# Two-layer decoder trunk on one core: second token tile's rows added ahead of the first tile's folding, attention's ScalarE and VectorE put into TensorE's order, inputs loaded and transposed tile by tile

## The chip, the cores and the metric

The kernel runs on one core of one Trainium2 chip. A core has TensorE (PE in the profile), VectorE (DVE), ScalarE (ACT), GpSimd (POOL) and SyncE (SP), which run their own instruction lists and meet through semaphores, and 16 DMA engines. The metric is the device time of one execution in microseconds (us). The profile is of one execution; its own time and its span are given below.

## The reference

Input x is 512 tokens by 1024 features in float32. Two layers, each a mixer and a mixture of experts (MoE), each followed by a layer norm of the residual:

```python
h = layer_norm(ALPHA * h + mixer(h)); h = layer_norm(ALPHA * h + moe(h))
```

Layer 0's mixer projects x by a 1024x1536 matrix; 512 of the columns feed a state-space branch (u), 1024 feed a gated convolution. Layer 1's mixer is a sparse attention with 16 heads over 4 key heads: per head a compressed branch (31 compressed keys), a selected branch and a window branch. With 512 positions all blocks are selected and the window covers all, so the last two are causal softmaxes over different keys and values. The MoE takes the top 8 of 64 experts plus one shared expert; every token gets eight expert rows, scaled by its gates, which are summed:

```python
y = sum over the 8 chosen experts of gate * ((silu(x @ w_gate[e]) * (x @ w_up[e])) @ w_down[e]) + shared(x)
```

## The kernel before

The program is a row of parts, each closed by a barrier: the even mixer (input projection, state space and convolution, finish), MoE layer 0, the odd mixer (input projection, compression, attention), MoE layer 1. The 512 tokens are four tiles (i = 0 to 3) of 128 partitions, all in float32. A float32 matmul stands in the profile as two MATMUL instructions.

**Input projection (`even_in_project`).** SP issues the loads in program order: the identity (first columns of the constant table), x in four tiles of 512 KB on one semaphore, the column constants, then the projection's weights in three pieces of 2 MB (`win[0]`, `win[2]`, `win[1]`, each of 512 columns), with the state matrices b and c between. PE waits for all of x, then transposes feature chunk by feature chunk over all four tiles (`emit_transposes`: eight groups of four transposes, two PSUM banks; ACT copies even chunks and DVE odd ones to `xT`), then makes twelve products of 16 MATMULs each in `order`, the first four from `win[0]`. DVE meanwhile builds tables, which PE transposes or multiplies between the later products.

**End of each MoE layer.** The expert rows were scattered to `y_dram`, eight rows per token. After the last step, SP issues 16 loads (`pieces`, 1 MB each, two of the eight rows of a tile's 128 tokens per piece, four pieces a tile, in tile order). For each tile DVE adds rows r = 0 to 3 to `g.x` (`add_row`, L850), and PE sums rows 4 to 7 in PSUM (`stored_rows`, L514) together with the rows of the last two steps, which it takes from SBUF by one-hot matmuls (`last_steps`, L522). `row_sums(i)` signals `half_done`. DVE then folds PE's sums in (L974, two instructions) and normalizes the tile (`norm.dve_tile`, with a square root on ACT). Before the loop (L968) DVE has added rows 0 to 2 of tile 0 (`EARLY` = 3). `row_sums(2)` and `row_sums(3)` wait until the banks that they reuse have been folded (L528). In layer 0 PE also transposes the normalized tiles (`turn_output`, L639); in layer 1 SP stores each tile to `out`.

**Attention (`attention`).** There are 32 units (`units`); unit n is a head pair's 128 queries, and its keys are 1, 2, 3 or 4 tiles of 128 (so unit n has "width" n % 4 + 1; the last four units run 4, 3, 2, 1). Each has four score blocks hb: two selected (hb 0, 1, in `bSel`) and two window (hb 2, 3, in `bWin`). For a block: PE makes scores, DVE adds the causal mask and takes the row minimum (`mask`, L2047), ACT takes the exponential and the row sum (L2021), DVE makes `coef` from the sums and gates (L2083), POOL scales (L1915), PE transposes (`turns`, L1954, PSUM banks `bT` in alternation, so a turn waits until the turn before the last has been copied out), ACT copies turns 0 and 2 and DVE turns 1 and 3 to `pT` (`take_turn`, L2009), and PE multiplies by the values (`values`, L1980). Once for each four units the compressed branch rides along: its scores come with the selected ones of a width-1 unit (L1932), DVE's `compressed_low` (three instructions, from L2054) and `compressed_scale` (L2067 to L2073) and one more turn (`compressed_turns`, L1962, copied by ACT at L2034) follow.

PE's order in iteration k is

```python
sel_scores(k + 1); turns(k - 2, 0); turns(k - 2, 1); compressed turn, if any
win_scores(k + 1); turns(k - 2, 2); turns(k - 2, 3); values(k - 3)
```

`sel_scores(k + 1)` waits until DVE has masked blocks 0 and 1 of unit k. ACT's order in its iteration k is the four exponentials of unit k, then turn 0 of unit k - 2, the compressed turn, turn 2. DVE's is the four masks of unit k, `coefficients(k - 1)`, then turns 1 and 3 of unit k - 2.

## Time and profile before

| | us |
|---|---|
| median of 3 runs | 2105.09 (2103.9 to 2106.59) |
| the profiled execution's own time | 2104.37 |
| its span in the trace | 2102.6 |
| PE busy | 1997.5 (95%) |
| DVE busy | 760.7 (36%) |
| ACT busy | 400.5 (19%) |
| POOL busy | 392.4 (19%) |

The granted TensorE clock averages 0.98 of full speed. The busy time of PE counts instructions whose modelled ends overlap the next one's start. The stages lie at 0 to 111 us (input projection), 113 to 207 (rest of the even mixer), 208 to 982 (MoE layer 0, its last rows from 922), 984 to 1329 (odd mixer, attention from 1142) and 1330 to 2102 (MoE layer 1, its last rows from 2040).

### The profile page before, as it was taken

How to read it: one execution, taken by the hardware profiler on the slowest of the kernel's cores; microseconds unless marked ns; L12 is line 12 of the kernel's file. 1: busy time of each engine (PE TensorE's matmuls, PEld its weight loads, DVE VectorE, ACT ScalarE, POOL GpSimd, SP SyncE). 2: the span in 40 equal slices, each digit the busy share in tenths (PEclk: the TensorE clock that was granted, in tenths of full speed). 3: DMA queues.
4: the chain of work that ended last, by engine and by line, in shares of the span. 5: the costliest groups of instructions: out<-in, count | busy, mean ns of one | idle time of the engine just before them, and what ended most of it. 6: DMA issues, size and time to landing. Idle time of an engine off the chain costs nothing. (4 is left out here: it accounts for less than half of the span.)

```text
span 2102.6 us, 26532 instructions
## 1 busy us (share of the span) xinstructions
PE 1997.5 (95%) x8566; PEld 994.1 (47%) x8566; DVE 760.7 (36%) x1957; ACT 400.5 (19%) x890; POOL 392.4 (19%) x379
## 2 busy tenths in 40 slices
PE   7998998999999999998998899998999999999997
PEld 4553454444444444444446565554444444444443
DVE  4683352222222222236532566343222222222226
ACT  2103021111111111111002566111111111111110
POOL 0000300111111111100110778500111111111110
PEclk9999999999999999999998899999999999999999
DMA  6133955999999999987402000656899999999977
GB/s 228 12 53 113 403 209 207 400 410 411 405 411 397 398 408 378 395 334 310 71 0 81 1 2 1 269 218 272 328 411 398 417 406 408 402 411 409 395 309 290
DMA packets 115169, 598.22 MB, mean 285 GB/s; under 512 B 38503, under 2 KB 39271, under 8 KB 76832
## 3 DMA queue, kind: packets, MB, share of 16 engines
q1 hardware_dynamic: 87456, 531.55, 63.6%
q0 software_dynamic: 27648, 65.82, 8.0%
q8 instruction: 40, 0.66, 0.1%
q14 instruction: 25, 0.20, 0.0%
HBM read 539.78 MB, written 91.23 MB: 300 GB/s over the span
## 5 line engine op out<-in xcount | busy, mean ns | idle before, releaser
L470 PE MATMUL moe_bank<-moe_weights,moe_xgT 128*128 128x512 f32 x1024 | 457.0, 599 | 16.4 <-DMA moe_weights<-in_ex_weights 16.0
L470 PEld LDWEIGHTS moe_bank<-moe_weights,moe_xgT 128*128 128x128 f32 x1024 | 189.9, 190 | 233.2 <-issue 215.9
L829 DVE TENSOR_TENSOR moe_hid<-moe_sil,moe_bank 128x256 f32<-128x256 f32 x98 | 41.3, 421 | 658.0 <-ACT moe_sil L692 658.0
L343 POOL DMA_INDIRECT y<-moe_xy,moe_rows x94 | 94.7, 1008 | 916.7 <-DVE moe_idx L809 501.2
L503 PE MATMUL moe_bank<-moe_weights,moe_hidT 128*128 128x512 f32 x512 | 230.5, 593 | 0.0
L473 PE MATMUL moe_bank<-wide,moe_xgT 128*64 128x512 f32 x512 | 226.6, 595 | 0.0
L473 PE MATMUL moe_bank<-moe_weights,moe_xgT 128*64 128x512 f32 x512 | 226.6, 595 | 0.0
L692 ACT ACTIVATE moe_sil<-moe_bank 128x256 f32<-128x256 f32 x98 | 37.7, 384 | 658.1 <-PE moe_bank L470 456.8
L328 POOL DMA_INDIRECT moe_xy<-h,moe_idx x98 | 99.9, 1019 | 267.7 <-DVE moe_idx L809 215.7
L837 DVE TENSOR_SCALAR moe_xy<-moe_bank,moe_sgate 128x512 f32<-128x512 f32 x98 | 73.5, 750 | 208.3 <-PE moe_bank L503 138.5
L1915 POOL TENSOR_SCALAR att_prob<-att_prob,att_coef 128x128 f32<-128x128 f32 (+3 forms) x128 | 136.8, 1090 | 60.4 <-DVE att_coef L2083 37.9
L503 PEld LDWEIGHTS moe_bank<-moe_weights,moe_hidT 128*128 128x128 f32 x512 | 92.4, 191 | 93.4 <-issue 93.4
L452 PEld LDWEIGHTS moe_bank<-const_sb,moe_xy 128*128 128x128 f32 x784 | 101.0, 192 | 66.9 <-issue 48.3
L473 PEld LDWEIGHTS moe_bank<-moe_weights,moe_xgT 128*64 128x64 f32 x512 | 67.5, 137 | 128.8 <-issue 127.9
L704 ACT ACTIVATE moe_xy<-moe_bank,moe_sgate 128x512 f32<-128x512 f32 x98 | 67.4, 687 | 290.8 <-PE moe_bank L503 190.7
L379 PE MATMUL moe_bank<-wide,xT 128*128 128x512 f32 x256 | 114.2, 602 | 7.6 <-PEq L46 7.6
L506 PE MATMUL moe_bank<-moe_weights,moe_hidT 128*64 128x512 f32 x256 | 116.7, 598 | 1.9 <-ACT moe_hidT L696 1.9
L506 PE MATMUL moe_bank<-wide,moe_hidT 128*64 128x512 f32 x256 | 116.7, 598 | 0.0
L452 PE MATMUL moe_bank<-const_sb,moe_xy 128*128 128x128 f32 x784 | 107.9, 281 | 9.1 <-DMA moe_xy<-h,moe_idx 9.1
L379 PEld LDWEIGHTS moe_bank<-wide,xT 128*128 128x128 f32 x256 | 48.5, 193 | 65.3 <-issue 65.3
L2021 ACT ACTIVATE att_prob<-att_prob,att_low 128x128 f32<-128x128 f32 (+3 forms) x128 | 70.4, 551 | 33.7 <-DVE att_low L2047 33.7
L822 DVE COPY moe_xgT<-moe_bank 128x512 f32<-128x512 f32 x98 | 67.8, 692 | 18.2 <-PE moe_bank L452 17.9
(357 smaller groups left out, 2460.2 us busy)
## 6 DMA issues: line engine op xcount, KB each, us to landing
moe_weights<-in_ex_weights SPq DMA_DIRECT2D x96, 2048.0 KB, 19.4
moe_weights<-in_ex_weights SPq DMA_DIRECT2D x96, 1024.0 KB, 17.7
wide<-in_ex_weights SPq DMA_DIRECT2D x34, 2048.0 KB, 21.8
wide<-in_ex_weights SPq DMA_DIRECT2D x34, 1024.0 KB, 14.7
y<-moe_weights SPq DMA_DIRECT2D x8, 4096.0 KB, 24.2
moe_weights<-y SPq DMA_DIRECT2D x16, 1024.0 KB, 19.2
wide<-y SPq DMA_DIRECT2D x8, 1024.0 KB, 14.4
oddin_win<-in_od_w_in_heads SPq DMA_DIRECT2D x1, 4288.0 KB, 19.9
```

The lines of the kernel that those rows point to most:

```text
L328: pool.indirect_dma_start(out=xg[k], out_offset=None, in_=h_dram[0:SEQ, :], in_offset=IndirectOffsetOnAxis(ap=idx[k][:, 0:1], axis=0), bou ...
L343: pool.indirect_dma_start(out=y_dram[:, :], out_offset=IndirectOffsetOnAxis(ap=rows[k][:, 0:1], axis=0), in_=y[k], in_offset=None, bounds_ ...
L379: mm = pe.matmul(bout[n % 4][:, :], g.xT[:, k, i * P:(i + 1) * P], g.wide[:, k, h * 512:(h + 1) * 512], start=(k == 0), stop=(k == KC - 1))
L452: mm = pe.transpose(bX[n // 4][:, (n % 4) * P:(n % 4 + 1) * P], xg[k].rearrange("t (k c) -> t c k", c=KC)[:, n, :], c["ident"])
L470: mm = pe.matmul(bG[:, :], xgT[:, n, :], wgu[j][:, :, n, :], start=(n == 0), stop=(n == KC - 1))
L473: mm = pe.matmul(bG[HP * h:HP * h + HP, :], xgT[:, n, HP * h:HP * h + HP], wgu[2 + h][:, :, n, :], start=(n == 0), stop=(n == KC - 1))
L503: mm = pe.matmul(bY[half][:, :], hidT[:, n, :], wdn[j][:, n, cols], start=(n == 0), stop=(n == HC - 1))
L506: mm = pe.matmul(bY[half][HP * h:HP * h + HP, :], hidT[:, n, HP * h:HP * h + HP], wdn[2 + h][:, n, cols], start=(n == 0), stop=(n == HC - 1))
L822: dve.tensor_copy(xgT[:, 4:8, :].rearrange("p k t -> p (k t)"), bX[1][:, :]).then_inc(xT_v, 1)
L837: dve.tensor_scalar(y[k][:, 512:1024], bY[1][:, :], sgate[k][:, 0:1], None, ALU.mult).then_inc(y_v, 1)
L1915: pool.tensor_scalar(prob[n % 4][:, hb, 0:width], prob[n % 4][:, hb, 0:width], coef[n % 3][:, hb:hb + 1], None, ALU.mult).then_inc(scaled, 1)
L2021: act.activation(prob[k % 4][:, hb, 0:width], prob[k % 4][:, hb, 0:width], ACT.Exp, scale=-1.0, bias=low[k % 2][:, hb:hb + 1], accum_out=t ...
```

## The change

There are three parts.

1. **MoE end.** `ON_DVE` becomes a number per tile, (4, 4, 4, 5): in tile 3 DVE adds rows 0 to 4 and PE rows 5 to 7. DVE adds tile 1's four rows before it waits for PE's half of tile 0, and none between the foldings of tiles 0 and 1. Both MoE layers run this code.
2. **Start.** Each tile of x has a semaphore. PE transposes a tile's eight chunks when that tile has landed, over four PSUM banks; ACT copies chunks 0 to 3 and DVE 4 to 7 of a tile, so four copies each, as before. `win[0]` is loaded as 256 columns (1 MB, with runs of 1 KB) directly behind x and ahead of the column constants, and its other 256 columns (1 MB) behind these; products 0 and 1 wait for the first, product 2 for the second. SP issues one transfer more.
3. **Attention.** PE's order stays. ACT's order becomes: turn 0 of unit k - 3, exponentials 0 and 1 of unit k, the compressed turn, turn 2 of unit k - 3, exponentials 2 and 3 of unit k. DVE's becomes: masks 0 and 1 of unit k, `compressed_low`, turn 1 of unit k - 3, masks 2 and 3, `coefficients(k - 1)`, `compressed_scale`, turn 3 of unit k - 3. The copy of the finished head output moves one iteration later on ACT, and `coefficients` gets a wait on DVE's own earlier instruction.

```diff
--- before.py
+++ after.py
@@ -154,7 +154,7 @@
         bX, bL, bG, bH, bY, bS = bank[0:2], bank[2], bank[3], bank[4], bank[5:7], bank[7]
         bsum = [bX, [bL, bS]]
         bout = bank[3:7]
-        ON_DVE, EARLY = 4, 3
+        ON_DVE, EARLY = (4, 4, 4, 5), 3
 
         loaded, shared_loaded, h_written = s.sem("router_loaded"), s.sem("shared_loaded"), s.sem("h_written")
         out_done, added = s.sem("out_done"), s.sem("out_added")
@@ -508,11 +508,11 @@
                 mm.then_inc(dn_done, 1)
 
             def stored_rows(i, first, final):
-                for r in range(ON_DVE, TOPK):
+                for r in range(ON_DVE[i], TOPK):
                     pe.wait_ge(landed[i][r // 2], 16)
                     for h in range(2):
                         mm = pe.matmul(bsum[i % 2][h][:, :], c["ident"], pieces[4 * i + r // 2][:, r % 2, h * 512:(h + 1) * 512],
-                                       start=(first and r == ON_DVE), stop=(final and r == TOPK - 1))
+                                       start=(first and r == ON_DVE[i]), stop=(final and r == TOPK - 1))
                 return mm
 
             def last_steps(i, first, final):
@@ -965,9 +965,12 @@
 
             norm.dve_begin(dve)
 
+            for r in range(EARLY, ON_DVE[0]):
+                add_row(0, r)
             for i in range(NT):
-                for r in range(0 if i else EARLY, ON_DVE):
-                    add_row(i, r)
+                for n in ((1,) if i == 0 else () if i == 1 else (i,)):
+                    for r in range(ON_DVE[n]):
+                        add_row(n, r)
                 dve.wait_ge(half_done, i + 1)
                 for h in range(2):
                     cols = slice(h * 512, (h + 1) * 512)
@@ -1159,8 +1162,9 @@
         tmp = [s.sb(f"tmp{k}", [P, QJ, LC + 1, GS]) for k in range(2)]
         mq = [s.sb(f"mq{k}", [P, 2, QJ, LC, GS]) for k in range(2)]
         bank = [s.ps(f"bank{k}", [P, 512]) for k in range(8)]
-        win_landed = [s.sem(f"win_landed{k}") for k in range(3)]
+        win_landed, first_landed = [s.sem(f"win_landed{k}") for k in range(3)], s.sem("first_landed")
         cols_loaded, bc_loaded, cleared, bdiag_ready = s.sem("cols_loaded"), s.sem("bc_loaded"), s.sem("cleared"), s.sem("bdiag_ready")
+        x_loaded = [s.sem(f"x_loaded{i}") for i in range(NT)]
         xt_done, xt_a, xt_v = s.sem("xt_done"), s.sem("xt_copied_act"), s.sem("xt_copied_dve")
         done, u_ready, u_stored, u_moved = s.sem("product_done"), s.sem("u_ready"), s.sem("u_stored"), s.sem("u_moved")
         sig_ready, h_ready = s.sem("sig_ready"), s.sem("h_ready")
@@ -1180,11 +1184,13 @@
 
             sp.dma_start(g.const_sb[:, 0:P], w["const_table"][:, 0:P]).then_inc(g.ident_loaded, 16)
             for i in range(NT):
-                sp.dma_start(g.x[:, i, :], w["x"][0, i * P:(i + 1) * P, :]).then_inc(g.x_loaded, 16)
+                sp.dma_start(g.x[:, i, :], w["x"][0, i * P:(i + 1) * P, :]).then_inc(x_loaded[i], 16)
+            src = w["ev_w_in"][0].rearrange("(p c) f -> p c f", c=KC)
+            sp.dma_start(win[0][:, :, 0:2 * P], src[:, :, 0:2 * P]).then_inc(first_landed, 16)
             sp.dma_start(e.cols[:], w["columns"]).then_inc(cols_loaded, 16)
-            src = w["ev_w_in"][0].rearrange("(p c) f -> p c f", c=KC)
             for k in (0, 2, 1):
-                sp.dma_start(win[k], src[:, :, k * 512:(k + 1) * 512]).then_inc(win_landed[k], 16)
+                lo = 0 if k else 2 * P
+                sp.dma_start(win[k][:, :, lo:], src[:, :, k * 512 + lo:(k + 1) * 512]).then_inc(win_landed[k], 16)
                 if k == 0:
                     sp.dma_start(e.b[:], w["b_states"]).then_inc(bc_loaded, 16)
                     sp.dma_start(e.c[:], w["c_states"]).then_inc(bc_loaded, 16)
@@ -1213,8 +1219,15 @@
         @block.tensor
         def _(pe):
             pe.wait_ge(g.ident_loaded, 16)
-            pe.wait_ge(g.x_loaded, 64)
-            emit_transposes(pe, g.x, g.c["ident"], bank[0:2], xt_done, (xt_a, xt_v))
+            for i in range(NT):
+                pe.wait_ge(x_loaded[i], 16)
+                if i >= 2:
+                    pe.wait_ge(xt_a, i - 1)
+                    pe.wait_ge(xt_v, i - 1)
+                for n in range(KC):
+                    mm = pe.transpose(bank[2 * (i % 2) + n // 4][:, (n % 4) * P:(n % 4 + 1) * P],
+                                      g.x[:, i, :].rearrange("t (k c) -> t c k", c=KC)[:, n, :], g.c["ident"])
+                mm.then_inc(xt_done, 1)
             pe.wait_ge(xt_a, 4)
             pe.wait_ge(xt_v, 4)
 
@@ -1242,7 +1255,9 @@
                 mm.then_inc(kern_done, 1)
 
             for n, f in enumerate(order):
-                if n in (0, 4, 5):
+                if n == 0:
+                    pe.wait_ge(first_landed, 16)
+                if n in (2, 4, 5):
                     pe.wait_ge(win_landed[f // 4], 16)
                 if 6 <= n < 10:
                     pe.wait_ge(u_ready, n - 5)
@@ -1259,9 +1274,9 @@
 
         @block.scalar
         def _(act):
-            for k in range(0, KC, 2):
-                act.wait_ge(xt_done, k + 1)
-                act.activation(g.xT[:, k, :], bank[0][:, :], ACT.Copy).then_inc(xt_a, 1)
+            for i in range(NT):
+                act.wait_ge(xt_done, i + 1)
+                act.activation(g.xT[:, 0:4, i * P:(i + 1) * P], bank[2 * (i % 2)][:, :].rearrange("p (k t) -> p k t", k=4), ACT.Copy).then_inc(xt_a, 1)
             act.wait_ge(cols_loaded, 16)
             act.activation(v["dt"][:], col["log_dt"], ACT.Exp).then_inc(dt_ready, 1)
             act.wait_ge(ldm_ready, 1)
@@ -1301,9 +1316,9 @@
 
         @block.vector
         def _(dve):
-            for k in range(1, KC, 2):
-                dve.wait_ge(xt_done, k + 1)
-                dve.tensor_copy(g.xT[:, k, :], bank[1][:, :]).then_inc(xt_v, 1)
+            for i in range(NT):
+                dve.wait_ge(xt_done, i + 1)
+                dve.tensor_copy(g.xT[:, 4:8, i * P:(i + 1) * P], bank[2 * (i % 2) + 1][:, :].rearrange("p (k t) -> p k t", k=4)).then_inc(xt_v, 1)
             link = lambda ins: dve_steps.link(dve, ins)
             mark = dve_steps.mark
             dve.wait_ge(cols_loaded, 16)
@@ -2011,30 +2026,38 @@
         @block.scalar
         def _(act):
             copy = lambda out, in_: act.activation(out, in_, ACT.Copy)
-            for k in range(units + 4):
+
+            def exponentials(k, hbs):
+                for hb in hbs:
+                    width = (where(k)[2] + 1) * P
+                    act.wait_ge(masked, 4 * k + hb + 1)
+                    if k >= 2 and hb == 0:
+                        act.wait_ge(coef_ready, k - 1)
+                    act.activation(prob[k % 4][:, hb, 0:width], prob[k % 4][:, hb, 0:width], ACT.Exp, scale=-1.0,
+                                   bias=low[k % 2][:, hb:hb + 1], accum_out=total[k % 2][:, hb:hb + 1]).then_inc(exp_ready, 1)
+
+            for k in range(units + 5):
+                turned = 3 <= k <= units + 2
+                if turned:
+                    take_turn(act, copy, k - 3, 0).then_inc(evac_a, 1)
                 if k < units:
-                    for hb in range(4):
-                        width = (where(k)[2] + 1) * P
-                        act.wait_ge(masked, 4 * k + hb + 1)
-                        if k >= 2 and hb == 0:
-                            act.wait_ge(coef_ready, k - 1)
-                        act.activation(prob[k % 4][:, hb, 0:width], prob[k % 4][:, hb, 0:width], ACT.Exp, scale=-1.0,
-                                       bias=low[k % 2][:, hb:hb + 1], accum_out=total[k % 2][:, hb:hb + 1]).then_inc(exp_ready, 1)
-                    for d in hosted(k):
-                        act.wait_ge(c_shifted, d + 1)
-                        flat = cp[d % 2][:].rearrange("p i h n -> p (i h n)")
-                        act.activation(flat, flat, ACT.Exp, scale=-1.0).then_inc(c_exp, 1)
-                if 2 <= k <= units + 1:
-                    take_turn(act, copy, k - 2, 0).then_inc(evac_a, 1)
-                    for d in c_turns(k):
+                    exponentials(k, (0, 1))
+                if turned:
+                    for d in c_turns(k - 1):
                         turn = turn_of["c", d]
                         act.wait_ge(t_done, turn + 1)
                         if d >= 2:
                             act.wait_ge(pv_done, NT * (d - 2) + 1)
                         copy(cpT[d % 2][:, :], bT[turn % 2][0:64, :]).then_inc(evac_a, 1)
-                    take_turn(act, copy, k - 2, 2).then_inc(evac_a, 1)
-                if k >= 7 and k % NT == 3:
-                    d = k // NT - 1
+                    take_turn(act, copy, k - 3, 2).then_inc(evac_a, 1)
+                if k < units:
+                    exponentials(k, (2, 3))
+                    for d in hosted(k):
+                        act.wait_ge(c_shifted, d + 1)
+                        flat = cp[d % 2][:].rearrange("p i h n -> p (i h n)")
+                        act.activation(flat, flat, ACT.Exp, scale=-1.0).then_inc(c_exp, 1)
+                if k >= 8 and k % NT == 0:
+                    d = k // NT - 2
                     pair, j, _ = where(NT * d)
                     act.wait_ge(pv_done, NT * d + NT)
                     copy(yT[:, NU * pair + j, :], bO[d % 2][:, :]).then_inc(o_copied, 1)
@@ -2076,6 +2099,8 @@
             def coefficients(n):
                 pair, j, i = where(n)
                 dve.wait_ge(exp_ready, 4 * n + 4)
+                if n:
+                    dve.wait_ge(coef_ready, n)
                 dve.reciprocal(inv[:], total[n % 2][:]).then_inc(inv_ready, 1)
                 dve.wait_ge(inv_ready, n + 1)
                 if n >= 3:
@@ -2086,7 +2111,7 @@
             first = a.gates[:, 0, :].rearrange("p (h b) -> p h b", b=3)[:, :, 0]
             dve.tensor_scalar(first, first, g.c["anycmp"], None, ALU.mult).then_inc(gate_ready, 1)
             dve.wait_ge(gate_ready, 1)
-            for k in range(units + 2):
+            for k in range(units + 3):
                 if k < units:
                     dve.wait_ge(sel_done, k + 1)
                     if k >= 4:
@@ -2097,6 +2122,9 @@
                     mask(k, 1)
                     for c, d in enumerate(hosted(k)):
                         compressed_low(d, c)
+                if 3 <= k <= units + 2:
+                    take_turn(dve, dve.tensor_copy, k - 3, 1).then_inc(evac_v, 1)
+                if k < units:
                     dve.wait_ge(win_done, k + 1)
                     mask(k, 2)
                     mask(k, 3)
@@ -2104,9 +2132,8 @@
                     coefficients(k - 1)
                     for d in hosted(k - 1):
                         compressed_scale(d)
-                if k >= 2:
-                    take_turn(dve, dve.tensor_copy, k - 2, 1).then_inc(evac_v, 1)
-                    take_turn(dve, dve.tensor_copy, k - 2, 3).then_inc(evac_v, 1)
+                if k >= 3:
+                    take_turn(dve, dve.tensor_copy, k - 3, 3).then_inc(evac_v, 1)
 
 
 
```

## Rows read from the trace of the kernel before

**Rows 1.** Timeline of PE, start: start us, length us, instructions, idle before and its releaser.
```profile
9.72 6.10 PE L83 MATMUL evin_bank<-const_sb,x_sb 128*128 128x128 f32 x28 [9.72 <-DMA x_sb<-in_x]
...
17.53 27.70 PE L1252 MATMUL evin_bank<-xT,wide 128*128 128x512 f32 x64 [0.83 <-issue]
```

**Rows 2.** Loads of x: ns of one issue, first and last start in us, then landing.
```profile
L1183 SPq DMA_DIRECT2D x_sb<-in_x x4: 421/428/443, 1.2 to 2.6; - x4
...
DMA to landing us min/median/max: 3.7/5.3/7.0
```

**Rows 3.** Windows, start: busy us of each engine, clock, DMA share, GB/s.
```profile
12.00:14.00 2.00, 2.00 (x10) 1.63 (x10) 0.79 (x2) 0.60 (x1) 0.00 (x0) 1.00 1.05 390
```

**Rows 4.** Timeline of DVE, end of MoE layer 1.
```profile
2060.50 1.28 DVE L974 TENSOR_TENSOR x_sb<-x_sb,moe_bank 128x512 f32<-128x512 f32 x2 [9.96 <-PE moe_bank L522]
...
2066.53 2.48 DVE L852 TENSOR_TENSOR x_sb<-x_sb,moe_weights 128x1024 f32<-128x1024 f32 x2
...
2071.56 1.29 DVE L974 TENSOR_TENSOR x_sb<-x_sb,moe_bank 128x512 f32<-128x512 f32 x2
...
2092.72 1.28 DVE L974 TENSOR_TENSOR x_sb<-x_sb,moe_bank 128x512 f32<-128x512 f32 x2
```

**Rows 5.** Timeline of PE, end of MoE layer 1.
```profile
2070.53 3.60 PE L522 MATMUL moe_bank<-moe_xy,moe_xgT 128*128 128x512 f32 x8
...
2084.26 7.03 PE L514 MATMUL moe_bank<-moe_weights,const_sb 128*128 128x512 f32 x16
```

**Rows 6.** Loads of the stored rows (pieces), layer 1: issue, then landing.
```profile
L286 SPq DMA_DIRECT2D moe_weights<-y x8: 432/442/2142, 2041.3 to 2055.1; - x8
...
DMA to landing us min/median/max: 4.8/16.5/28.8
```

**Rows 7.** Timeline of PE, end of MoE layer 0.
```profile
952.39 3.60 PE L522 MATMUL moe_bank<-moe_xy,moe_xgT 128*128 128x512 f32 x8
```

**Rows 8.** Timeline of DVE, end of MoE layer 0.
```profile
953.71 1.28 DVE L974 TENSOR_TENSOR x_sb<-x_sb,moe_bank 128x512 f32<-128x512 f32 x2
```

**Rows 9.** Groups by line, attention, PE: busy us, mean ns, idle before and releasers.
```profile
L1924 PE MATMUL att_bSel<-odd_ksT,odd_qT 64*128 64x128 f32 (+3 forms) x128 | 28.8, 529 | 11.0 <-DVE att_low L2047 7.9 <-DVE att_cprob L2054 1.8 <-PEq L46 1.2
```

**Rows 10.** Timeline of one round of four units, PE, DVE and ACT.
```profile
1198.95 0.92 PE L1924 MATMUL att_bSel<-odd_ksT,odd_qT 64*128 64x384 f32 x4 [0.31 <-DVE att_low L2047]
...
1204.60 1.13 PE L1924 MATMUL att_bSel<-odd_ksT,odd_qT 64*128 64x512 f32 x4 [0.27 <-DVE att_low L2047]
...
1206.91 0.60 PE L1962 MATMUL att_bT<-const_sb,att_cprob 128*64 128x128 f32 x4 [0.81 <-ACT att_pT L2013]
...
1207.54 0.59 ACT L2013 ACTIVATE att_cprobT<-att_bT 64x512 f32<-64x512 f32 x1 [0.78 <-PE att_bT L1962]
...
1209.18 0.68 DVE L2047 CUSTOM_DVE_ANT_0 att_prob<-att_bSel,const_sb 128x512 f32<-128x512 f32 x1
...
1209.90 0.72 ACT L2021 ACTIVATE att_prob<-att_prob,att_low 128x512 f32<-128x512 f32 x1 [0.76 <-DVE att_low L2047]
...
1210.76 0.49 PE L1924 MATMUL att_bSel<-odd_ksT,odd_qT 64*128 64x128 f32 x4
```

**Rows 11.** Timeline, end of that round.
```profile
1214.67 0.42 DVE L2054 TENSOR_TENSOR att_cprob<-att_bSel,const_sb 128x256 f32<-128x256 f32 x1
...
1220.13 0.92 PE L1924 MATMUL att_bSel<-odd_ksT,odd_qT 64*128 64x384 f32 x4 [0.31 <-DVE att_low L2047]
```

**Rows 12.** Timeline of POOL, last five units.
```profile
1302.20 23.16 POOL L1915 TENSOR_SCALAR att_prob<-att_prob,att_coef 128x512 f32<-128x512 f32 x20 [0.42 <-ACT att_prob L2021]
```

**Rows 13.** Windows, fifth unit of attention: columns as in rows 3.
```profile
1162.00:1164.00 2.00, 0.40 (x7) 0.35 (x8) 1.91 (x6) 1.24 (x4) 0.00 (x0) 1.00 0.00 0
1164.00:1166.00 2.00, 1.85 (x24) 1.41 (x20) 1.18 (x7) 2.00 (x7) 0.72 (x1) 0.77 0.00 0
```

**Rows 14.** Timeline of PE, units 4 and 6 (selected scores).
```profile
1163.65 0.49 PE L1924 MATMUL att_bSel<-odd_ksT,odd_qT 64*128 64x128 f32 x4 [1.60 <-DVE att_low L2047]
...
1177.88 0.92 PE L1924 MATMUL att_bSel<-odd_ksT,odd_qT 64*128 64x384 f32 x4 [0.31 <-DVE att_low L2047]
```

## Prediction

> **What bounds the kernel now.** I read the page first. PE is busy for 95% of the span, so most of the time is matmul time that the change doesn't touch, and what it can win are stretches where PE is idle or is not the last to finish. I then took PE's timeline at the three places of the change, with those of DVE, ACT and POOL beside it.
>
> At the start, PE does nothing until 9.72, when all of x is in; the transposes then take until 16.7, in step with copies, and the first product starts at 17.53 [rows 1]. From there PE runs without a gap through the projection.
>
> At the end of each MoE layer DVE is idle 9.96 us before it folds tile 0 [rows 4]. It has no idle after that: it goes from folding to norm to the next rows. The last folding starts at 2092.72, and what follows it (norm, store) ends the kernel. But PE's sums are hardly earlier: its half of tile 1 ends where the next L522 starts, 2070.53 [rows 5], and a folding can begin 0.27 later (L522 of tile 0 handed over that way at 2060.50), so at 2070.8, against the folding at 2071.56 [rows 4]. DVE is ahead of PE by 0.76 us of slack, no more.
>
> In attention, PE loses 11.0 us before the selected scores, nearly all to DVE's masks [rows 9], and the rest of its waits go to ACT's copies of turns, such as 0.81 us before each compressed turn [rows 10]. One round of four units takes 21.18 us (1198.95 to 1220.13) [rows 10, 11].
>
> **Start.** The tiles are issued at 1.2 to 2.6 and take 3.7 to 7.0 us to land [rows 2], so they land at about 4.9, 6.5, 8.1 and 9.65. The 32 transposes have 7.0 us in [rows 1] including waits for copies; eight without waits are about 1.6 us (estimate: a quarter of the 28 in 6.10 us). Tile by tile: tile 0 is transposed 4.9 to 6.5, tile 1 to 8.1, tile 2 to 9.7, tile 3 to 11.3. Its two copies (0.6 to 0.7 us, the number and size of copies are unchanged) end at about 12.2. The copies of earlier tiles hide under the transposes of the next. The second condition is the first half of `win[0]`: 1 MB behind x at 390 GB/s [rows 3] is 2.7 us, from 9.65 to 12.35. So product 0 starts at about 12.4 instead of 17.53: **-5.1 us**. Product 2 needs the other half at 12.4 + 13.9 = 26.3 (a product is 27.70 / 4 = 6.9 us); with 172 KB of columns ahead it lands at 15.5. The extra issue is 0.43 us on SP and hidden by the transfers. The columns land some 2.7 us later than now, and DVE is free 5 us earlier, so its tables move forward too; everything else in the stage hangs on PE, which has no gap, so the gain reaches the stage's end. Bounds: if 1 KB runs went at half rate, the half lands at 15.0 and the gain is 2.4; if PE were ready at once, 5.3. I take 5.1, since PE's own chain and the transfer arrive together. The trace shows no load with 1 KB runs at this rate.
>
> The Trainium skill (DMA: Bandwidth & Descriptors, the table of key figures) says that transfers of 512 B and more go at line rate, by which the half would land at 12.35; no run here shows it yet.
>
> **MoE end.** Tile 1's adds need pieces 4 and 5. Pieces land in order; the first at 2040.0 + 4.8 = 2044.8, the sixteenth at 2055.1 + 28.8 = 2083.9 [rows 6], 2.6 us apart, so piece 5 lands at about 2057.9 and the four adds end at 2060.4, just in time for tile 0's folding at 2060.50. If they came up to 4 us later nothing would be lost. Folding 0 and norm 0 end at 2066.53 as now [rows 4]. Then DVE waits for PE until 2070.8: folding 1 moves from 2071.56 by only 0.76, though 5.0 us of adds were taken away in front of it. The rest turns into an idle of 4.3 us. From there tile 2 is as now (adds 5.0, folding and norm 5.55), and tile 3 has a fifth add, 2.48 / 2 = 1.24 us. PE's sum of tile 3 ends at 2091.3 now [rows 5] and 1.7 us earlier after, but DVE isn't there yet: its folding 3 comes at 2092.72 - 0.76 + 1.24 = 2093.2. So the fifth add goes onto the path and the part as a whole is **+0.5 us** in layer 1. In layer 0 the same sum has 953.71 - (952.39 + 0.27) = 1.05 us of slack [rows 7, 8]: -1.05 + 1.24 = **+0.2 us**. Bounds for both layers: -1.8 (the fifth add free) to +2.5 (no slack gained at all).
>
> **Attention.** I follow one round, with the durations of rows 10 and 11 and those between them: masks start 0.61 us apart at width 4 (0.21 at width 1), exponentials 0.71 (0.40), PE hands over to DVE in 0.11, ACT to PE in 0.14. I call an iteration by the width of the unit whose scores it makes.
>
> Width 3 (now 5.65: 1198.95 to 1204.60). Masks 0 and 1 now run beside the turns instead of behind turn 3, so the 0.27 before the next scores goes. But `compressed_scale` of the iteration before ends late, and turn 1 waits 0.2. New: 5.4.
>
> Width 4 (now 6.16: 1204.60 to 1210.76). The 0.81 before the compressed turn shrinks to 0.35, since turn 0 no longer waits behind four exponentials. But the compressed copy (0.59) now stands behind exponentials 0 and 1: mask 0 gives at +1.9, exponentials to +3.3, copy to +3.9, and turn 3, which takes its bank, waits from +3.6 to +4.05. New: 6.15, no gain.
>
> Width 1 (now 4.68: 1210.76 to 1215.44). On DVE turn 1 now stands behind masks 0 and 1 and the three instructions of `compressed_low` (0.42 each [rows 11], 1.3 in all): its copy is ready at +3.55 where turn 3 could go at +2.5. New: 5.45, which is 0.8 worse.
>
> Width 2 (now 4.69). All waits go (0.37 for ACT, 0.31 for DVE): 3.95.
>
> Round: 20.95 against 21.18. So PE's old waits are swapped for new ones, and five and a bit rounds at full clock give **-1.6 us**. Two places gain more. Unit 4's scores wait 1.60 us for masks that stand behind turn 3 of unit 0 [rows 14]; the new order has them done long before: **-1.6**. And in the last five units POOL works through 20 scalings without a gap, 23.16 us from 1302.20 [rows 12]; it starts when `coefficients(27)` is done, now about 1.5 us behind the end of PE's iteration 27, after the change 0.4 before it (masks 2 and 3 no longer wait for turn 3). Everything behind follows: **-2.0**. Attention: **-5.2**. Bounds: all of PE's waits gone would be 2 us a round, some -16 in all; a wait of 1 us more in each round than I find, +3.
>
> **Sum.** -5.1 + 0.2 + 0.5 - 5.2 = -9.6. The profiled execution has 2104.37 (span 2102.6), 0.7 under the median of 2105.09; the median becomes 2095.5.
>
> **Rivals.**
>
> *TensorE's clock doesn't fall a second time.* It is granted 1.00 at 1162 to 1164, where PE is busy 0.40 of 2 us, and falls in the next 2 us (0.77) [rows 13], to 0.5 of full, 1.2 GHz. The stretch from unit 4 to unit 6 takes 14.23 us [rows 14] where the same two iterations take 9.37 at full clock (1210.76 to 1220.13), 4.9 more. The change fills that hole of 1.60 us. If the clock then stays up: 2095.5 - 4.9 = 2090.6. Against it: at 1142 to 1161 the clock was low with busier stretches, and there are still waits in unit 4. Chance 0.2.
>
> *Attention gives nothing.* If the two new waits are larger than I find (turn 1 behind `compressed_low`, turn 3 behind the compressed copy), by 0.8 us a round in all seven, the 5.2 are eaten: 2100.7. Chance 0.17.
>
> *The first weights are late.* At half rate for 1 KB runs: 2095.5 + 2.7 = 2098.2. Chance 0.1.
>
> *Slower: the new wait of 1.05 us in each width-1 iteration takes the clock down.* There are six such units with turns in flight. One fall costs 4.9 (above), so six cost 29: 2125. Two falls cancel the whole gain, three make it slower. Against it: in the old rounds holes of 0.81 us leave the clock up, and PE is busy before and behind. For it: the one hole of 1.60 us was followed by a fall. Chance 0.06.
>
> The Trainium skill (TensorE: Matmul & The Clock Gate, "A second HAM failure mode: psum-queue depth-cycling") reports short idles between groups of matmuls that let the clock swing between its two levels; by it this last rival would be 2125, and the trace has so far one fall that fits.
>
> **How the numbers follow.** The likeliest, 2095.5, has 0.45; 0.02 is left for what I don't see. A measurement here tells 0.2% (4.2 us) from no change, so faster means under 2100.9. Likeliest, clock and late weights are faster (0.75), and of the attention rival a third: 0.80. The rest of that rival and some of the unseen are the same: 0.13. Slower: 0.07. The range goes from a little under the clock rival to a little over the attention one: 2089 to 2102.
>
> **What would show it.** Start: the first L1252 at about 12.4, and no wait before the third product. MoE end: DVE idle some 4 us before the second L974, and the last L974 later relative to PE's first L514 by 0.5. Attention: rounds of about 21.0; no wait of selected scores for masks, instead waits of L1954 for ACT and DVE in width-4 and width-1 iterations; POOL's last 20 scalings some 2 us nearer to unit 28's scores. I would be wrong if the rounds came to 19 or to 22, if the clock row at unit 4 stayed 1.00, or if `half_done` came earlier than the sums above.

## The result and the profile after

The changed kernel takes 2093.61 us (median of 6 runs, 2089.53 to 2096.53), the kernel before 2104.49 (6 runs, 2103.26 to 2106.59). The ratio is 0.9945, 95% interval 0.9932 to 0.9959: 10.9 us or 0.55% faster. The profiled execution has 2092.64 of its own, span 2090.8, mean granted clock 0.982.

The stages, each measured between the first instructions of PE's lines, say where the time went (us, before and after). The two MoE ends are counted from PE's first matmul on the stored rows (L514):

| stretch | before | after |
|---|---|---|
| span's start to product 0 | 17.5 | 13.1 |
| attention: first scores to MoE 1 | 188.6 | 180.2 |
| end of MoE 0: first L514 to the odd mixer | 52.9 | 53.2 |
| end of MoE 1: first L514 to the last norm | 47.3 | 47.7 |

These four make -12.1, and the spans differ by -11.8. The other stretches, which the change doesn't touch, sum to +0.3, but singly they differ more: MoE layer 1 up to its first L514 is 3.1 us longer (719.2 before, 722.3 after), MoE layer 0 up to there 1.5 shorter and the state-space part 1.7 shorter.

Start, timeline of PE in the kernel after (start, length, line, shapes, idle before and releaser), and then its x copy on DVE:

```profile
5.69 6.57 PE L1228 MATMUL evin_bank<-const_sb,x_sb 128*128 128x128 f32 x32 [5.69 <-DMA x_sb<-in_x]
13.09 27.70 PE L1267 MATMUL evin_bank<-xT,wide 128*128 128x512 f32 x64 [0.83 <-DVE xT L1321]
```
```profile
12.30 0.69 DVE L1321 COPY xT<-evin_bank 128x512 f32<-128x512 f32 x1 [0.52 <-PE evin_bank L1228]
```

PE begins 4.0 us earlier than in [rows 1], at tile 0. Product 0 waits for DVE's last copy, not for the weights, and from it 64 matmuls run with no gap, the third product's among them.

End of layer 1, DVE and PE:

```profile
2042.66 2.48 DVE L852 TENSOR_TENSOR x_sb<-x_sb,moe_weights 128x1024 f32<-128x1024 f32 x2 [4.32 <-DMA moe_weights<-y]
...
2048.31 1.28 DVE L977 TENSOR_TENSOR x_sb<-x_sb,moe_bank 128x512 f32<-128x512 f32 x2 [0.65 <-PE moe_bank L522]
...
2058.54 1.29 DVE L977 TENSOR_TENSOR x_sb<-x_sb,moe_bank 128x512 f32<-128x512 f32 x2 [4.13 <-PE moe_bank L514]
...
2069.12 1.28 DVE L977 TENSOR_TENSOR x_sb<-x_sb,moe_bank 128x512 f32<-128x512 f32 x2
...
2079.70 1.22 DVE L852 TENSOR_TENSOR x_sb<-x_sb,moe_weights 128x1024 f32<-128x1024 f32 x1
2080.96 1.28 DVE L977 TENSOR_TENSOR x_sb<-x_sb,moe_bank 128x512 f32<-128x512 f32 x2
```
```profile
2058.34 3.60 PE L522 MATMUL moe_bank<-moe_xy,moe_xgT 128*128 128x512 f32 x8
...
2072.08 5.31 PE L514 MATMUL moe_bank<-moe_weights,const_sb 128*128 128x512 f32 x12
```

The 9.96 us in front of the first folding [rows 4] have shrunk, as the adds of tile 1 fill them. Part of what was freed stands behind it: DVE waits 4.13 us for PE's sum of tile 1. The foldings are now 10.23, 10.58 and 11.84 us apart (the first gap was 11.06), and the last gap is the one with a fifth add in it.

Attention, PE's groups over the whole stage (idle before, and what ended it):

```profile
L1969 PE MATMUL att_bT<-const_sb,att_prob 128*128 128x128 f32 x320 | 52.7, 290 | 9.0 <-DVE att_pT L2024 4.5 <-POOL att_prob L1930 2.0 <-ACT att_cprobT L2028 1.7
...
L1939 PE MATMUL att_bSel<-odd_ksT,odd_qT 64*128 64x128 f32 (+3 forms) x128 | 28.6, 527 | 5.8 <-DVE att_low L2070 2.8 <-DVE att_cprob L2077 1.8 <-PEq L46 1.2
...
L1977 PE MATMUL att_bT<-const_sb,att_cprob 128*64 128x128 f32 x32 | 5.2, 289 | 2.7 <-ACT att_pT L2028 2.7
```

The scores' wait for masks falls from 7.9 us [rows 9] to 2.8 and is one single wait, before unit 3's scores. The turns now wait 4.5 us for DVE. One round, to be laid beside [rows 10]:

```profile
1185.89 0.92 PE L1939 MATMUL att_bSel<-odd_ksT,odd_qT 64*128 64x384 f32 x4
...
1191.09 1.13 PE L1939 MATMUL att_bSel<-odd_ksT,odd_qT 64*128 64x512 f32 x4
...
1192.94 0.60 PE L1977 MATMUL att_bT<-const_sb,att_cprob 128*64 128x128 f32 x4 [0.35 <-ACT att_pT L2028]
...
1195.15 0.30 PE L1969 MATMUL att_bT<-const_sb,att_prob 128*128 128x128 f32 x1 [0.29 <-ACT att_cprobT L2028]
...
1197.29 0.49 PE L1939 MATMUL att_bSel<-odd_ksT,odd_qT 64*128 64x128 f32 x4
...
1200.88 0.41 PE L1969 MATMUL att_bT<-const_sb,att_prob 128*128 128x128 f32 x2 [0.91 <-DVE att_pT L2024]
...
1206.77 0.92 PE L1939 MATMUL att_bSel<-odd_ksT,odd_qT 64*128 64x384 f32 x4
```

What PE waits for at 1200.88 stands on DVE: the copy of turn 1 comes behind the last instruction of `compressed_low`.

```profile
1199.98 0.42 DVE L2084 TENSOR_TENSOR att_cprob<-att_cprob,att_clow 128x256 f32<-128x256 f32 x1
1200.32 0.41 DVE L2024 COPY att_pT<-att_bT 128x256 f32<-128x256 f32 x1
```

The round takes 20.88 us (1185.89 to 1206.77) against 21.18. The next round takes 22.38, and the windows say why (columns as in [rows 3]; the granted clock is the third number from the end):

```profile
1220.00:1222.00 2.00, 1.09 (x9) 0.68 (x8) 1.93 (x11) 1.44 (x7) 2.00 (x2) 1.00 0.00 0
1222.00:1224.00 2.00, 2.00 (x12) 0.86 (x10) 0.60 (x5) 1.50 (x6) 1.91 (x2) 0.84 0.05 12
1224.00:1226.00 2.00, 2.00 (x10) 1.32 (x9) 0.69 (x3) 0.00 (x0) 2.00 (x3) 0.50 0.00 0
1226.00:1228.00 2.00, 2.00 (x14) 1.29 (x12) 1.20 (x6) 1.56 (x6) 2.00 (x2) 0.81 0.00 0
```

Behind the new wait of 0.91 us the granted clock goes to 0.50 of full, 1.2 GHz, and comes back within 5 us. At the front of the stage it is the other way round. First the kernel before, then the kernel after, 20 us each:

```profile
1140.00:1160.00 20.00, 14.13 (x70) 8.33 (x72) 10.85 (x47) 8.70 (x29) 5.71 (x8) 0.53 0.54 211
1160.00:1180.00 20.00, 17.58 (x102) 10.11 (x102) 9.95 (x42) 10.27 (x33) 12.78 (x11) 0.70 0.00 0
```
```profile
1140.00:1160.00 20.00, 14.50 (x69) 6.96 (x70) 15.41 (x65) 12.85 (x46) 9.98 (x11) 0.71 0.37 148
1160.00:1180.00 20.00, 18.46 (x172) 12.05 (x171) 12.95 (x52) 12.70 (x42) 17.81 (x18) 1.00 0.01 2
```

The time at 1.2 GHz can be summed over windows of 1 us: each counts with twice the part of the clock that is missing in it. By that sum attention has 30.7 us at 1.2 GHz before, in pieces of 20.5 and 10.3 that end at 1176. After, it has 10.2 and 6.8 in front and 3.4 in a round, 20.4 in all; another 3.4 lie about the start of MoE 1.

In the last five units POOL's 20 scalings now start at 1286.90, 0.36 us ahead of the width-3 scores at 1287.26; before they started 1.63 us behind them (1302.20 [rows 12] and 1300.57):

```profile
1286.90 23.14 POOL L1930 TENSOR_SCALAR att_prob<-att_prob,att_coef 128x512 f32<-128x512 f32 x20 [0.57 <-DVE att_coef L2108]
```

### The profile page after: what moved, and what is told of

Its sections match the earlier page's. It is cut to its first block and busy times, and to the rows that moved or that the text cites. A ratio compares the mean times of both kernels' runs of the same rounds, so it can differ in the third digit from the quotient of the medians.

```text
span 2090.8 us, 26554 instructions
## 1 busy us (share of the span) xinstructions
PE 1993.8 (95%) x8558; PEld 993.9 (48%) x8558; DVE 761.9 (36%) x1959; ACT 399.4 (19%) x890; POOL 394.6 (19%) x379
## 5 line engine op out<-in xcount | busy, mean ns | idle before, releaser
L470 PE MATMUL moe_bank<-moe_weights,moe_xgT 128*128 128x512 f32 x1024 | 460.4, 603 | 13.6 <-DMA moe_weights<-in_ex_weights 13.2
```

Of the source, the lines that this page charges most:

```text
L470: mm = pe.matmul(bG[:, :], xgT[:, n, :], wgu[j][:, :, n, :], start=(n == 0), stop=(n == KC - 1))
```

## Experiments

**The three parts alone.** Each kernel has only the hunks of one part: the start (loads, transposes, copies, `first_landed`), the folding (`ON_DVE` and the tile 1 adds), or attention.

> Only the start part of the change is made (x tile by tile, first weights in halves). My account: the profile of the changed kernel has the first product at 13.1 us instead of 17.5, and nothing behind it in the stage waits, so this part alone is worth 4.4 us. The span up to the first out-product of MoE layer 0 is 4.4 shorter, give or take 2 us of clock at the stage boundaries. Rival: the 4.4 us are taken back at a later wait (the loads of the state space part, or the weights that the MoE loop waits for), and the kernel is within 1 us of before.

> Only the MoE end is changed. From L514's first start to L982's or the last norm instruction, my sums give +0.2 us in layer 0 and +0.5 us in layer 1: PE's half of tile 1 limits the gain to its slack and the fifth row of tile 3 is on DVE's path. Kernel: +0.7 us, not to be told from no change by the median. Rival: rows added ahead give back the 5 us per layer that DVE no longer spends behind tile 0's norm, and the kernel is 5 to 10 us faster.

> Only attention's orders are changed. The prediction's sum was -5.2 with the second fall of the clock kept, -10.1 without it. Rounds of 20.9 against 21.18, POOL's last 20 scalings start 2 us earlier relative to the scores of unit 28, unit 4's scores 1.6 earlier. If the clock at unit 4 stays up in this profile too, the attention stage is 8 to 10 us shorter; if it falls as before, 5. Rival: the gain of the changed kernel's attention stage (8.4) came from where its clock windows happened to lie and not from the order, and then this one differs from it by several us in the same stage.

> The changed kernel again, beside its parts. If the parts add up, it is the sum of the three: about -4.4 + 0.7 - 8 = -12 us. Its six runs lay 7 us apart (2089.5 to 2096.5) where those of before lay 3.3 apart. Theory: the new wait of 0.9 us in each width-1 iteration of attention lets the clock fall now and then (once in the first profile, in the round that took 22.38 instead of 20.87), so the number and place of falls differs between executions. Rival: the spread comes from the MoE loops' weight loads, and this profile's attention stage is the same length as the first's.

| kernel | median us (range of runs) | ratio to before, 95% | product 0, us | attention, us |
|---|---|---|---|---|
| start_only | 2097.99 (2096.08 to 2102.75) | 0.9966 (0.9954 to 0.9979) | 12.5 | 189.2 |
| fold_only | 2105.32 (ten runs, 2103.57 to 2109.49; two more took 2383.43 and 4174.0) | 1.0001 (0.9992 to 1.001) | 17.3 | 189.2 |
| att_only | 2096.83 (2094.33 to 2099.51) | 0.9957 (0.9944 to 0.997) | 16.9 | 182.1 |
| whole_again | 2090.34 (2089.0 to 2093.37) | 0.9934 (0.9921 to 0.9947) | 12.0 | 180.2 |

The kernel before had 2105.35 beside them. The parts add up: -7.4, 0 and -8.5 make -15.9 against -15.0 for the whole, where -12 was expected and the first measurement gave -10.9.

The profile of the start alone has 5.0 us less in front of product 0, and MoE layer 0 begins 5.3 us earlier; the other 2 us of its median are within its interval (-9.7 to -4.4). Here product 0 waits 1.35 us for the weights, where in the profile of the whole change it waited for the last copy. So the two conditions are as close together as the forecast had them.

The folding alone has the same ends of the MoE layers as the whole change, 53.2 and 47.7 us. Attention alone is 6.5 us shorter (188.6 to 182.1), where 8 to 10 were expected. Its front is like that of the whole change (30.1 us from the first scores to unit 6's); what it lacks is a longer fall of the clock in one round, 6.8 us, and that round takes 24.06.

The two profiles of the whole change differ by 3.6 us, and none of it lies in attention, which has 180.2 and one fall of 3.4 us in a round in both. MoE layer 1 up to its first L514 takes 722.3 in one and 717.4 in the other, with 13.7 and 3.4 us at 1.2 GHz from 1310 us on. So for these two executions the theory of the expectation (falls in attention make the spread) doesn't hold. The spread comes mostly from MoE layer 1, and there from the clock more than from the weight loads, for which PE waits 6.7 and 6.5 us.

**The fifth add, and one tile ahead everywhere.** Two edits of the folding, the first measured in one execution only.

```
four_rows:  ON_DVE, EARLY = (4, 4, 4, 4), 3
one_ahead:  for n in ((i + 1,) if i + 1 < NT else ()):
```

> The whole change with four rows on DVE in tile 3 as in the others (4, 4, 4, 4). My account says that the fifth add is on the path: the stretch from PE's first L514 to the last norm instruction in layer 1, 47.3 us before and 47.7 with the change, becomes 46.5 (0.76 of slack gained, nothing given back); in layer 0 DVE's last folding comes 1.0 us after PE's signal limit, 0.7 earlier than before the change. Rival: tile 3's folding waits for PE with four rows (PE sums one row more, 1.7 us) and the stretch stays at 47.7 or grows.

> The whole change with DVE one tile ahead all the way: tile 1's rows before folding 0, tile 2's before folding 1, tile 3's five rows before folding 2. DVE's hole of 4.1 us before folding 1 is filled. By my sums foldings come at 2060.5, 2071.6, 2083.4 and 2089.7 on the clock of the kernel before (PE's half of tile 3 is the last to come), so the stretch from the first L514 to the last norm instruction is 47.3 - 3.0 = 44.3 instead of 47.7, and in layer 0 about 3 us shorter too (stored rows to odd projection 50 instead of 53). Kernel: 6 us faster than the change. Rival: the pieces of tiles 2 and 3 land too late for adds that early (2.6 us a piece), DVE then holds back folding 1 and PE's reuse of its banks, and the stretch is not under 47.

four_rows: 2091.83, end of layer 1 46.4 us in place of 47.7. So the fifth add costs its whole 1.3; in layer 0 it costs 1.1 (52.1 in place of 53.2). one_ahead: 2092.13 (ratio 0.9938, 0.9919 to 0.9957), end of layer 1 44.1 us and of layer 0 51.1. Its foldings on DVE:

```profile
2053.46 1.29 DVE L977 TENSOR_TENSOR x_sb<-x_sb,moe_bank 128x512 f32<-128x512 f32 x2 [0.64 <-PE moe_bank L522]
...
2064.51 1.28 DVE L977 TENSOR_TENSOR x_sb<-x_sb,moe_bank 128x512 f32<-128x512 f32 x2
...
2076.35 1.29 DVE L977 TENSOR_TENSOR x_sb<-x_sb,moe_bank 128x512 f32<-128x512 f32 x2
...
2082.57 1.28 DVE L977 TENSOR_TENSOR x_sb<-x_sb,moe_bank 128x512 f32<-128x512 f32 x2 [0.59 <-PE moe_bank L514]
```

The 4.13 us hole is gone, and at the last folding DVE waits for PE again: 6.22 us lie between the last two. The two ends are 3.6 and 2.1 us shorter than with the change, where 3.4 and 3 were expected. The 6 us expected for the kernel don't show in the median, which is 1.5 under the first measurement of the whole change and 1.8 over the second. Its profiled execution has 34.1 us at 1.2 GHz in and about attention against 23.9, and its attention takes 183.8 us against 180.2, which takes the gain of layer 1 back; whether the other runs did the same isn't known.

**The two new waits of attention.** turn1_first moves one line of DVE, copy_first one exponential of ACT, both_waits has both edits.

```
turn1_first (DVE):
   mask(k, 1)
+  take_turn(dve, dve.tensor_copy, k - 3, 1).then_inc(evac_v, 1)
   for c, d in enumerate(hosted(k)):
       compressed_low(d, c)
-  take_turn(dve, dve.tensor_copy, k - 3, 1).then_inc(evac_v, 1)
copy_first (ACT):
-  exponentials(k, (0, 1))
+  exponentials(k, (0,))
   ...  # compressed copy
+  exponentials(k, (1,))
   take_turn(act, copy, k - 3, 2).then_inc(evac_a, 1)
```

> The whole change, with DVE copying turn 1 before compressed_low in attention instead of behind it. My account: the wait of 0.91 us before turn 3 in width-1 iterations goes, a round falls from 20.87 to 19.95, six rounds give 5.5 us: attention stage 175 instead of 180.2. Rival: compressed_low, later now, pushes masks 2 and 3 and coefficients, so that PE waits as long elsewhere (the next turn 1 or POOL's scalings), and a round stays above 20.6.

> The former, and on ACT the compressed copy between exponentials 0 and 1 instead of behind 1. My account: the waits of 0.35 before the compressed turn stay, that of 0.29 before turn 3 goes too; rounds of 19.65, attention stage 173, kernel 7 us faster than the change. If the hole of 0.91 us is what lets the clock fall within the rounds, no fall comes behind the third round and the runs lie closer together. Rival on the clock: falls come as often with the hole gone, since what matters is PE's small matmuls and not that one hole.

> The whole change with only ACT's side mended: the compressed copy between exponentials 0 and 1, compressed_low still ahead of turn 1 on DVE. The 0.29 before turn 3 in width-4 iterations goes, the 0.91 in width-1 iterations stays; rounds of 20.58. On the clock: if the hole of 0.91 us is what lets it fall, this one shows a fall within the rounds as the five profiles with the hole did; if the 0.29 did it, none.

turn1_first took 2088.84 (one execution), with 174.6 us of attention and rounds of 19.77. copy_first took 2087.87 (one execution), with 178.1 and rounds of 20.51. both_waits took 2082.19 (2079.61 to 2086.16, ratio 0.9888, 0.9873 to 0.9904), with 169.8. A round of both_waits, PE:

```profile
1187.23 0.92 PE L1939 MATMUL att_bSel<-odd_ksT,odd_qT 64*128 64x384 f32 x4
...
1194.28 0.60 PE L1977 MATMUL att_bT<-const_sb,att_cprob 128*64 128x128 f32 x4 [0.35 <-ACT att_pT L2028]
...
1206.51 0.92 PE L1939 MATMUL att_bSel<-odd_ksT,odd_qT 64*128 64x384 f32 x4
```

It takes 19.28 us with one wait in it, and so do the round before it and each of the three behind it; the clock stays at 1.00 in all of them. The two waits cost 1.6 us a round (20.88 less 19.28), and the fall came on top.

Copy_first doesn't fit the simple reading that the 0.91 us hole, PE's idle time before turn 3, makes the clock fall. It keeps that hole in each round, and its clock doesn't fall in any:

```profile
1200.90 0.41 PE L1969 MATMUL att_bT<-const_sb,att_prob 128*128 128x128 f32 x2 [0.91 <-DVE att_pT L2024]
```
```profile
1200.00:1202.00 2.00, 1.10 (x4) 0.49 (x4) 1.76 (x9) 1.44 (x8) 2.00 (x3) 1.00 0.00 0
1202.00:1204.00 2.00, 2.00 (x17) 1.21 (x17) 0.37 (x3) 0.66 (x2) 2.00 (x2) 1.00 0.00 0
```

**First weights in one piece.** The whole change, but `win[0]` as one load of 2 MB, and no wait of its own for the third product.

```
-  sp.dma_start(win[0][:, :, 0:2 * P], src[:, :, 0:2 * P]).then_inc(first_landed, 16)
+  sp.dma_start(win[0], src[:, :, 0:512]).then_inc(first_landed, 16)
   ...  # the second half's load and the third product's wait go
```

> The whole change, with the first weights in one load of 2 MB (products 0 to 3 wait for all of it). Theory: the halves matter, since PE has x transposed by 12 us and 2 MB behind x need 5.4 us from 9.0 to 9.7, so product 0 starts at 14.6 to 15.2 instead of 12.0 to 13.1. Rival: runs of 1 KB made the halves no faster than the whole, and product 0 starts as early as with them.

The one execution took 2115.08, longer than any of the kernel before (up to 2110.95 beside it). The start is as expected, product 0 at 14.4:

```profile
4.96 6.27 PE L1228 MATMUL evin_bank<-const_sb,x_sb 128*128 128x128 f32 x32 [4.96 <-DMA x_sb<-in_x]
14.36 16.17 PE L1267 MATMUL evin_bank<-xT,wide 128*128 128x512 f32 x30 [3.13 <-DMA wide<-in_ev_w_in]
```

What was not expected is the clock. In attention it is low for 6.8 us in each of five rounds, though the attention code is the same as after. The stage takes 193.0 us. Windows of three rounds:

```profile
1190.00:1198.00 8.00, 7.49 (x30) 4.08 (x31) 3.30 (x17) 3.18 (x12) 7.33 (x5) 0.58 0.01 2
1198.00:1214.00 16.00, 14.96 (x146) 10.07 (x145) 10.75 (x41) 10.38 (x32) 9.96 (x12) 1.00 0.01 2
1214.00:1222.00 8.00, 7.49 (x29) 3.97 (x30) 3.20 (x17) 3.18 (x12) 7.33 (x5) 0.57 0.00 0
1222.00:1238.00 16.00, 14.93 (x147) 10.05 (x145) 10.88 (x41) 10.41 (x32) 9.96 (x12) 1.00 0.01 2
1238.00:1246.00 8.00, 7.52 (x29) 3.92 (x30) 3.11 (x17) 3.15 (x12) 7.30 (x5) 0.57 0.01 3
```

The same kernel was run again, in six runs:

> The same kernel as unsplit: the whole change, but win[0] is loaded in one piece of 2 MB; its one look took 2115.08, with TensorE at half clock for 6.8 us in every round of attention. Theory A (the phase at which the clock is looked at differs from one execution to the next): its runs scatter from about 2092 to 2115, and the median lies nearer 2095, that is 2091 plus 1.3 to 2.4 for the later start. The new profile then shows falls in one round or none. Theory B (the later start fixes when attention's waits come, so that they meet the clock badly in every execution): all runs are near 2110 to 2115, and the new profile again shows 6.8 us at half clock in each round. The new waits of 0.91 us are in both.

Its median is 2098.03 (2093.86 to 2104.63; ratio 0.9972, 0.9955 to 0.9988), and its profile, which is of the slowest of the six, has one fall of 3.4 us in the rounds, attention 183.9. So theory B is out: the same program spent 34 us of its rounds at half clock in one execution and 3.4 in another. That it goes by the phase, as theory A has it, isn't shown. None of the six runs came near 2115, and they ran on another chip than the first execution, so chip and execution aren't told apart here. But copy_first, with the same holes, ran on the chip of the first execution and had no fall.

Its median is 4.4 and 7.7 us over the two of the split version; the interval of its ratio overlaps that of the first a little and that of the second not at all. The start comes 1.4 to 2.5 us later, and the windows of unsplit_again show more behind it:

```profile
10.00:15.00 5.00, 1.31 (x9) 0.93 (x8) 1.12 (x2) 1.03 (x3) 0.00 (x0) 1.00 1.05 382
15.00:20.00 5.00, 5.00 (x9) 2.11 (x8) 4.43 (x14) 2.26 (x5) 1.59 (x4) 0.66 1.04 387
```

PE waits 3.69 us for the 2 MB, and then the clock falls for 3.4 us. In the first execution of this kernel it falls for 6.8 us, and begins while PE still waits, at 13 to 14:

```profile
13.00:21.00 8.00, 6.64 (x9) 2.81 (x10) 5.54 (x15) 2.36 (x5) 1.59 (x4) 0.57 1.05 383
```

From product 0 to the next stage it takes 97.5 us in unsplit_again and 98.8 in unsplit, against 95.7 or 95.8 in each other kernel. MoE layer 0 up to its first L514 is longer in both as well, 725.7 and 725.8 us against 721.4 to 724.3 in the others; why isn't known.

**The best of it.** both_waits and one_ahead together.

> The change with both waits of attention mended and DVE one tile ahead through the whole MoE end. The parts: 2082 for the first, and 3.6 us (layer 1) and 2.1 us (layer 0) less for the second: 2076.5 us. Rounds of 19.28, stretch from the first L514 to the last norm instruction 44.1, no clock fall within the rounds behind the third. Rival: the shorter stages only move waits to the weight loads of the MoE loops, and the median stays within 2 us of 2082.

It takes 2080.55 us (2077.66 to 2081.81, ratio 0.988, 0.986 to 0.990), 25 us less than before and faster than the changed kernel. Attention takes 170.0 and the end of layer 1 44.1; in the profile both edits keep what they gave. 2076.5 was expected, and the median is only 1.6 under that of both_waits, with overlapping intervals. That is where the rival had it, within 2 us of 2082; its cause, waits that move to the weight loads, isn't shown by any run. How much the folding order gives in time isn't settled.

## Why the prediction was right

The forecast was 2095.5 in a range of 2089 to 2102, and the kernel takes 2093.6. The sum of -9.6 stands against -10.9 in the medians (-15.0 in the second measurement) and -11.7 in the profiled executions' own times. The start and the MoE ends came as reasoned. In attention one step failed, and the number is nearer than the parts because two things that the sum did without pull against each other: 4.3 us more gained at the front of the stage, 1.5 lost to a fall in a round. That they left the time so close to 2095.5 is luck.

**Start: -5.1 predicted, -4.4 in that profile, -5.0 in the start alone.** The mechanism is as written, with PE's chain and the transfer close together. The half load is issued at 3.1 and lands after 9.4, at 12.5 (12.35 predicted), under the copy that ends at 12.99. In start_only it is the other way round, and PE waits for the half load until 12.45. (The upper bound of the gain, 5.3, should read 5.2: 17.53 less 12.35.) The late-weights rival is out: 1 MB in 1 KB runs lands at the full rate. The term that was off is the arrival of tile 0, 4.9 by my reading and 5.69 here; in other executions it is 4.96 and 5.21. The Trainium skill (DMA: Bandwidth & Descriptors, Specifications) puts the least transfer for line rate at 512 B, and the trace agrees: 12.5 us. What I left out is a second use of the split: without it PE has a hole of 3.1 to 3.7 us, and the clock fell for 3.4 and 6.8 us in the two executions, which cost 1.7 and 3.0 more.

**MoE end: +0.2 and +0.5 predicted, +0.3 and +0.4 measured.** The hole of 4.3 us came as 4.13, and the fifth add costs 1.3 (four_rows). That 5 us of work taken from in front of a folding moves it by less than 1 is confirmed: the second folding comes 10.23 us behind the first instead of 11.06, and the folding alone is at 1.0001.

**Attention: -5.2 predicted, -8.4 measured, in three pieces.** By starts of PE's lines:

| piece | predicted | before | after | difference |
|---|---|---|---|---|
| first scores to unit 6's | -1.6 | 35.9 | 30.0 | -5.9 |
| unit 6 to the last unit of width 3 (1300.57 before) | -1.6 | 122.7 | 122.2 | -0.5 |
| from there to MoE 1 | -2.0 | 30.0 | 28.0 | -2.0 |

Three rows after that bound the pieces, and 1.92 us of the last is PE's own queue, as before:

```profile
1165.04 0.92 PE L1939 MATMUL att_bSel<-odd_ksT,odd_qT 64*128 64x384 f32 x4
...
1287.26 0.92 PE L1939 MATMUL att_bSel<-odd_ksT,odd_qT 64*128 64x384 f32 x4
...
1315.27 21.25 PE L379 MATMUL moe_bank<-wide,xT 128*128 128x512 f32 x45 [1.92 <-PEq L46]
```

The round was right, 20.95 predicted and 20.88 measured, and so were its waits: 0.35 before the compressed turn, 0.29 for the compressed copy, and 0.91 (1.05 predicted) for turn 1 behind `compressed_low`. The tail was right to 0.1, and by its reason: POOL's last 20 scalings start 2.0 us nearer to the scores.

**The step that failed** is in the first piece: the sum let the clock fall a second time at the front of the stage, as before. The wait of 1.60 us [rows 14] is gone, and so is the fall behind unit 4's scores [rows 13]: 1160 to 1180 is granted 1.00 in place of 0.70. I had named that as a sign of being wrong. The piece gave 5.9 us instead of 1.6, so it was mis-sized by 4.3. That is close to the clock rival (-6.5 with the wait), to which I had given 0.2.

That the filled wait is what kept the clock up is not shown. For it: the three profiles with the old order (before, start_only, fold_only) have 30.7 us at 1.2 GHz at the front, and the eleven with a new one 13.6 to 27.3 (17.0 in the changed kernel). Against it: in one_ahead and unsplit_again, 17.1 us of low clock follow the first 10.2, although the 1.60 us wait is gone there too. One window of one_ahead, with PE busy 18.28 of 20 us:

```profile
1150.00:1170.00 20.00, 18.28 (x80) 10.27 (x81) 10.19 (x43) 11.01 (x36) 15.34 (x13) 0.57 0.01 2
```

So the gain at the front differs with the execution.

In the second piece five rounds gave 1.4 us, one fall took 1.5 back (22.38 against 20.88), and the last units of the piece gave 0.5. The term itself holds a slip: five and a bit rounds at 0.23 (21.18 less 20.95) are 1.2, not 1.6. The fall is the mechanism of the rival that I had put on the slower side. It is real, but its price was wrong: I took 4.9 from the front of the stage, where the low stretch is 10.3 us long; in a round it is mostly 3.4 us long and costs 1.5, and the rounds with 6.8 us take 24.0, 3.1 more. The Trainium skill (TensorE: Matmul & The Clock Gate, "A second HAM failure mode: psum-queue depth-cycling") reports of another kernel, in bf16, that PE idles shortly between groups of matmuls often enough for the clock to swing between its two levels. The rows at 1220 to 1228 agree, and one execution of unsplit swings in each round and is slower than the kernel before; copy_first has the same idles and doesn't swing.

**What stays open** is when the hole is followed by a fall. Of the eight profiles that have 0.91 us in each round, six have one fall in the rounds, of 3.4 us or (att_only) 6.8 (after, whole_again, att_only, four_rows, one_ahead, unsplit_again), unsplit has five and copy_first none. The three without it (turn1_first, both_waits, best) and the three with the old order (before, start_only, fold_only) have none in the rounds, only some 3.4 us in the tail or at the start of MoE 1 in the first three. The eight profiles have 40 such holes and 11 falls in the rounds, and each fall begins within 2 us of a hole's end. By all that was run the hole is needed for a fall in the rounds, but it isn't enough. That it hangs on when in the execution the hole comes was argued, not shown.

## What to carry to other kernels

Before a stall is filled by moving an instruction ahead on the same engine, follow for a whole round what now has to stand behind it. Here the change of order took attention from 188.6 to 180.2 us, and two small reorderings within DVE's and ACT's queues took it further to 169.8: 1.6 us a round, and no falls in the rounds in the two profiles that have both.

Adds taken from in front of a step gain only the slack of the engine that hands over last. With the adds of every tile done one tile ahead, that stretch was 3.6 us shorter.

Where PE has regular short holes, one profile doesn't tell the time: read the granted clock round by round, and measure in several executions.

## What the runs showed of the hardware

- In and about attention the low clock came in stretches of 3.4, 6.8, 10.2, 17.1 and 20.5 us in these profiles. One of 3.4 us in a round cost 1.5 us, one of 6.8 us 3.1.
- A PE hole of 3.1 to 3.7 us at the start, after about 6 us of transposes, came with a fall in both executions that had it (granted 0.66 in 15 to 20 us in one, 0.57 in 13 to 21 in the other). The kernel before, which leaves PE idle until 9.72 and then waits for copies, has none there (1.00 from 10 to 25 us).
- A PE hole of 0.91 us was followed by a fall within 2 us in 11 of 40 cases, five of them in one execution.
- The same program, with the same code in attention, took 183.9 and 193.0 us for that stage in two executions, on two chips.
